# Stick-breaking sums from two rounded halves, a later sparse tail, and an early start of the mixing-out projection

## The chip, the cores and the metric

The kernel is one program on one core of a Trainium2 chip. The metric is the device time of one execution in microseconds; the time before is the median of three runs. Its engines are TensorE (PE, with the weight load PEld), VectorE (DVE), ScalarE (ACT), GpSimd (POOL) and SyncE (SP).

## The reference, cut to what matters

Two transformer blocks run in f32 on 512 tokens of width 1024. The change lies in the second, in its attention stage. There, eight heads do sparse attention and eight do stick-breaking attention; both outputs are joined and projected:

```python
def stick_breaking(q, k, v):                       # 8 heads of 64
    z = jnp.einsum('bhqd,bhkd->bhqk', qb, k) * scale      # qb: 128 queries
    mask = kpos[None, :] < tq[:, None]
    log_rem = jnp.where(mask, jax.nn.log_sigmoid(-z), 0.0)
    suffix = lax.cumsum(log_rem, axis=3, reverse=True) - log_rem
    a = jnp.where(mask, jnp.exp(jax.nn.log_sigmoid(z) + suffix), 0.0)
    return jnp.einsum('bhqk,bhkd->bhqd', a, v)

x = x + jnp.concatenate([o_nsa, o_sb], axis=-1) @ w_out
x = x + memory_cross_attention(rms_norm_2(x, ...), ...)
```

Since log_sigmoid(z) = z - softplus(z), the exponent is z minus the sum of softplus over this key and all later ones. With keys on the partitions that sum is a product of a triangle of minus ones with the softplus values of the same block of 128 keys, plus a product of a full block of minus ones with those of each later block.

## The kernel before, in words

Activations lie transposed, features on the partitions, as eight chunks `[128, 512]`. A projection multiplies in three rounded products (fp32r), high by high, low by high and high by low (`mm3`, L415 to L417): `xh`, `xl` are the halves of the activations, `wh`, `wl` those of the weights. ScalarE makes the high half of a weight unit (L341), VectorE the low half (L353); both work one unit ahead. Semaphores order the engines, and each engine runs its instructions in the order in which they are written.

The attention stage is `pe_second_attention`, `act_second_attention` and `dve_second_attention` (from L2203). One loop over `s` runs first over 24 sparse jobs, then over ten stick-breaking units, with `n = s - 24`. A sparse job passes through scores (step s), turn (s + 1: products with a diagonal, L688, then copies, L707 and L714) and attend (s + 2, L723); the last of three jobs is put into `xh` and `xl` (L730, L733). These outputs fill chunks 0 to 3, those of stick-breaking 4 to 7.

A stick-breaking unit holds, for two heads, four blocks of keys by 128 queries, thus 1024 columns: query block 3 of one pair of heads, or blocks 0 and 2 of one pair, or block 1 of two pairs. Among the ten units there are four, four and two of these. The order on TensorE in round n is

- scores(n): 16 small products (L2089) and the mask (L2094), into one of three pairs of banks (0 and 1, 2 and 3, 4 and 5); they wait for the exponential of unit n - 3, which reads the same banks;
- sums(n - 2): f32 products of minus ones with the later blocks (L2143, L2147) and with the triangle (L2148), added onto the scores;
- attend(n - 3): 16 products with the values (L2172) into bank 6 or 7, waiting for the VectorE put of unit n - 5.

ScalarE in round n: absolute value of scores(n) (L2103), exponential of unit n - 2 (L2157), the two steps of the log for n (L2107, L2109), the high-half put of unit n - 4 (L730). VectorE: softplus of n (L2121), the additions of later blocks (L2128 to L2133; two, one or none), the low-half put of unit n - 4 (L733).

`pe_mix_out` (L1228) then multiplies eight output tiles c of 128 features, each of eight chunks by three products of 512 columns, in banks 0 and 1 by turns. For tile c it waits for the residual addition of tile c - 2 (L738). The first block's mixing-out ("out") already starts with chunks 0 to 3 beside the attention; the second's ("out2") does not. `pe_memory` follows, with its two query projections in banks 2 and 3.

Of the kernel before, what the change touches and what calls it, by code (L numbers as in the profile page):

```python
# [7 lines left out]
ALU = mybir.AluOpType  # L8
# [151 lines left out]
def program(nc, A, out, tables):  # L160
    ctx = ExitStack()
    with ctx:
# [115 lines left out]
        pr2 = sb("pr2", [P, 2, 4, T], F32, part)  # L278
        pt2 = sb("pt2", [P, 2, 4 * T], F32, part)
        part.close()  # L280
        second.close()
# [944 lines left out]


        def pe_mix_out(e, name, stage):  # L1228
            for n in range(4):
                u = of[name, n]  # L1230
                e.wait_ge(*WLO[u])
                for cc in range(2):
                    c = 2 * n + cc
                    if c > 1:
                        e.wait_ge(*VF[name, "residual", c - 2])
                    k0 = 4 if n == 0 and name == "out" else 0
                    pe_proj(e, c % 2, u, cc * P, xh, xl, stage if c == 0 else None, NC - k0, k0, k0 == 0, kw=k0).then_inc(
                        *MM.up((name, "out", c), *([("w", u)] if cc else [])))
                pe_finish(e, u)
# [9 lines left out]
        def dve_mix_out(e, name, coef, each=None):  # L1249
            for n in range(4):  # L1250
                dve_ahead(e, of[name, n])
                for c in (2 * n, 2 * n + 1):
                    dve_residual(e, name, c, c % 2, coef(c))
# [857 lines left out]
        def dve_stick_logs(e, n):  # L2111

            par = n % 2
            e.wait_ge(*EX["log", n])
            if n < 2:
# [3 lines left out]
            i, o = (3, 0) if len(STICK[n]) == 1 else (2, P)  # L2119
            last = [("stick", "sums", n)]  # L2120
            e.scalar_tensor_tensor(out=zs[par], in0=stick_scores(n), scalar=0.0, in1=ze[par], op0=ALU.max, op1=ALU.add).then_inc(  # L2121
                *VS.up(("stick", "soft", n), *(last if STICK[n][0][1] == 1 else [])))
            if STICK[n][0][1] == 1:
                return
            z, u = (x[par].rearrange("p (y t) -> p y t", y=2) for x in (zs, zu))
            e.wait_ge(*VS["stick", "soft", n])
            if i == 3:
                e.tensor_tensor(u[:, :, P:2 * P], z[:, :, 2 * P:3 * P], z[:, :, 3 * P:4 * P], ALU.add).then_inc(  # L2128
                    *VS.up(("stick", "later", n)))
                e.wait_ge(*VS["stick", "later", n])  # L2130
                e.tensor_tensor(u[:, :, 0:P], z[:, :, P:2 * P], u[:, :, P:2 * P], ALU.add).then_inc(*VS.up(*last))
            else:
                e.tensor_tensor(u[:, :, 0:P], z[:, :, 2 * P:3 * P], z[:, :, 3 * P:4 * P], ALU.add).then_inc(*VS.up(*last))  # L2133

        def pe_stick_sums(e, n):
            par = n % 2
            e.wait_ge(*VS["stick", "sums", n])
            for y in range(2):
                s, z = (x[:, y * 512:(y + 1) * 512] for x in (stick_scores(n), zs[par]))
                u = zu[par][:, y * 256:(y + 1) * 256]  # L2140
                for c, i, o in stick_entries(n):
                    if i > 1:
                        e.matmul(s[:, o:o + (i - 1) * P], b2("neg1"), u[:, 0:(i - 1) * P], start=False, stop=False,  # L2143
                                 skip_group_check=True)
                    if i:
                        a = o + (i - 1) * P
                        e.matmul(s[:, a:a + P], b2("neg1"), z[:, a + P:a + 2 * P], start=False, stop=False, skip_group_check=True)  # L2147
                m = e.matmul(s, b2("tri"), z, start=False, stop=True, skip_group_check=True)  # L2148
            m.then_inc(*MM.up(("stick", n)))
# [42 lines left out]
        def dve_stick_put(e, n):  # L2192
            dst, src = stick_places(n, xl)
            e.wait_ge(*AX["stick", n])
            dve_put(e, dst, src, stick_places(n, xh)[0], ("stick", n), *([("mix2", c) for c in range(NC)] if n == NU - 1 else []))

# [6 lines left out]
        def pe_second_attention(e):  # L2203
# [4 lines left out]
            for s in range(NN + NU + 3):  # L2208
# [7 lines left out]
                elif 2 <= n < NU + 2:  # L2216
                    pe_stick_sums(e, n - 2)
                if 1 < s < NN + 2:
                    J = nsa_[s - 2]
                    if J.first and J.n:  # L2220
                        e.wait_ge(*VX["nsa", J.n - 1, 1])
                    pe_attend(e, J)
                elif n >= 3:
                    pe_stick_attend(e, n - 3)

        def act_second_attention(e):
            for s in range(NN + NU + 4):
# [11 lines left out]
                if 0 < s <= NN:  # L2239
                    act_turn(e, nsa_[s - 1])  # L2240
                if 1 < s < NN + 2:
                    J = nsa_[s - 2]
                    if J.last:
# [7 lines left out]
        def dve_second_attention(e):  # L2251
            for s in range(NN + NU + 4):
# [7 lines left out]
                if s < NN:  # L2260
                    dve_scale(e, nsa_[s])
                if 1 < s < NN + 2:
                    J = nsa_[s - 2]
                    if J.last:
                        for o in range(2):
                            r, cs, cols, src = nsa_places(J, o)
                            e.wait_ge(*AX["nsa", J.n, o])
                            dve_put(e, xl[r, cs, cols], src, xh[r, cs, cols], ("nsa", J.n, o))
                elif n >= 4:
# [23 lines left out]
        def pe_memory(e):  # L2293
            u = of["mq"]
            e.wait_ge(*WLO[u])
            pe_proj(e, 2, u, 0, nh, nl, "n5").then_inc(*MM.up(("in2", "qm0")))
            e.wait_ge(*VF["square", "out2", 7])
            pe_sums(e, "out2", ssum, 1, T)
            pe_proj(e, 3, u, P, nh, nl, nk=4, stop=False)
            pe_head_sums(e, "qm0", 0, 8, VF["token term", "out2"])  # L2300
            pe_proj(e, 3, u, P, nh, nl, nk=4, k0=4, kw=4, start=False).then_inc(*MM.up(("in2", "qm1"), ("w", u)))
            pe_head_spread(e, "qm0", 1, T, 6)
# [33 lines left out]
        def act_memory(e):  # L2336
            act_head_in(e, "qm0", 2, qm[:, 0, :], 0)
            act_head_root(e, "qm0", 1)
            act_ahead(e, of["mq"])
            act_head_in(e, "qm1", 3, qm[:, 1, :], 1)  # L2340
            act_head_root(e, "qm1", 2)
# [288 lines left out]
```

## Time and profile before

| | us |
|---|---|
| median of three runs (2232.75 to 2236.04) | 2235.04 |
| the profiled execution | 2237.97 |
| its span, first to last instruction | 2236.1 |
| stretch from the first stick-breaking scores to the first mixing-out product | 1709.1 to 1776.4 |

The span and all the rows are of the one profiled execution. A row of the timeline gives start, length and line; several instructions of one kind are merged (x16). The length of a TensorE row includes the time in which its last product drains, so that the next row begins before it ends: the step from start to start is the time that the array takes. The time in brackets is idle time before, and what ended it.

### The profile page before, as it was taken

The numbers are of one execution on the slowest core, as the hardware profiler recorded it, in microseconds if no ns is written. First come the engines' busy times: TensorE is split into PE (matmuls) and PEld (weight loads), VectorE is DVE, ScalarE is ACT, GpSimd is POOL, SyncE is SP. The second block draws the span as 40 slices with busy tenths as digits, with TensorE's granted clock in tenths as the row PEclk, the third lists the DMA queues.
The fourth block names the chain that finished last, engine by engine and source line by source line (L and its number), as shares of the span: only waits on it lengthen the run. The fifth ranks groups of instructions, "written<-read, shape, count | busy, mean of one in ns | idle before, by whom it ended". The sixth has DMA issues, their size and how long they took to land.

```text
span 2236.1 us, 26468 instructions
## 1 busy us (share of the span) xinstructions
PE 2163.9 (97%) x11362; PEld 1776.0 (79%) x11362; DVE 1049.0 (47%) x1381; ACT 746.4 (33%) x1125; POOL 78.5 (4%) x76
## 2 busy tenths in 40 slices
PE   6989989999998999999999999999999999999999
PEld 4778778888887888888888888877777677888887
DVE  5758565555536333333533333363375357333322
ACT  4335332222233222232322322333356545222211
POOL 0000000000000000000111100000000002111000
PEclk9999999999998999999999999999899999999999
DMA  9421445555531333323233323333100021333232
GB/s 356 132 83 39 151 132 191 190 170 196 179 105 57 94 94 101 100 86 109 87 102 94 95 85 104 104 92 113 57 1 1 20 75 57 94 100 105 93 96 78
DMA packets 190901, 236.03 MB, mean 106 GB/s; under 512 B 4096, under 2 KB 175392, under 8 KB 190656
## 3 DMA queue, kind: packets, MB, share of 16 engines
q1 hardware_dynamic: 189696, 230.42, 32.1%
q0 software_dynamic: 1088, 3.92, 0.5%
q8 instruction: 90, 1.47, 0.3%
q14 instruction: 27, 0.22, 0.0%
HBM read 231.31 MB, written 2.10 MB: 104 GB/s over the span
## 4 chain that ended last, share of the span: by engine, by line
PE 86%; DVE 6%; ACT 4%; DMA 1%; SPq 1%; issue 1%; DVEq 0%; ACTq 0%
PE ps L415 25%; PE ps L417 25%; PE ps L416 25%; PE ps L688 3%; PE ps L618 2%; PE ps L723 1%; ACT pr L647 1%; DVE wl L353 1%; SPq L782 1%; PE ps L394 1%; DVE tmp L547 1%; ACT wh L341 1%; PE ps L508 1%; DMA mmT<-in_ada_w 1%; PE ps L459 1%
## 5 line engine op out<-in xcount | busy, mean ns | idle before, releaser
L415 PE MATMUL ps<-xh,wh 128*128 128x512 f32 x1768 | 697.7, 395 | 17.7 <-DVE xl L559 8.0
L416 PE MATMUL ps<-xl,wh 128*128 128x512 f32 x1768 | 691.4, 391 | 0.0
L417 PE MATMUL ps<-xh,wl 128*128 128x512 f32 x1768 | 691.3, 391 | 0.0
L353 DVE TENSOR_TENSOR wl<-raw,wh 128x2048 fp32r<-128x2048 f32 (+2 forms) x169 | 376.8, 2230 | 488.7 <-ACT wh L341 488.6
L341 ACT CAST wh<-raw 128x2048 fp32r<-128x2048 f32 (+1 forms) x170 | 314.5, 1850 | 339.9 <-PE ps L417 254.0
L415 PEld LDWEIGHTS ps<-xh,wh 128*128 128x128 f32 x1768 | 333.2, 188 | 93.5 <-issue 14.6
L417 PEld LDWEIGHTS ps<-xh,wl 128*128 128x128 f32 x1768 | 333.0, 188 | 70.7
L416 PEld LDWEIGHTS ps<-xl,wh 128*128 128x128 f32 x1768 | 333.2, 188 | 70.1 <-issue 1.4
L415 PE MATMUL ps<-hh,wh 128*128 128x512 f32 x704 | 274.3, 390 | 0.0
L417 PE MATMUL ps<-hh,wl 128*128 128x512 f32 x704 | 274.1, 389 | 0.0
L416 PE MATMUL ps<-hl,wh 128*128 128x512 f32 x704 | 274.1, 389 | 0.0
L1351 ACT CAST hh<-tmp 128x512 fp32r<-128x512 f32 x88 | 54.7, 621 | 328.7 <-DVE tmp L1405 328.7
L417 PEld LDWEIGHTS ps<-hh,wl 128*128 128x128 f32 x704 | 132.2, 188 | 27.4
L415 PEld LDWEIGHTS ps<-hh,wh 128*128 128x128 f32 x704 | 132.2, 188 | 27.3
L416 PEld LDWEIGHTS ps<-hl,wh 128*128 128x128 f32 x704 | 132.2, 188 | 27.2
L1405 DVE TENSOR_TENSOR tmp<-ps,tmp 128x512 f32<-128x512 f32 x88 | 60.8, 691 | 140.3 <-PE ps L417 137.2
L367 DVE SCALAR_TENSOR_TENSOR acc<-raw,sc,acc 128x1024 f32<-128x1024 f32 x70 | 89.9, 1284 | 40.7 <-DMA raw<-in_ada_w 39.2
L688 PE MATMUL ps<-tmp,pr 128*128 128x128 f32 (+1 forms) x736 | 98.2, 290 | 5.1 <-DVE tmp L671 4.1
L647 ACT ACTIVATE pr<-ps,sm 128x512 f32<-128x512 f32 (+5 forms) x144 | 72.6, 513 | 80.0 <-DVE sm L634 44.5
L688 PEld LDWEIGHTS ps<-tmp,pr 128*128 128x128 f32 (+1 forms) x736 | 89.0, 193 | 9.0 <-DVE tmp L671 5.9
L733 DVE TENSOR_TENSOR hl<-tmp,hh 128x512 fp32r<-128x512 f32 x88 | 60.9, 693 | 60.5 <-ACT hh L1351 60.5
L1432 POOL TENSOR_TENSOR tmp<-tmp,acc 128x512 f32<-128x512 f32 x44 | 56.8, 1292 | 802.3 <-ACT tmp L1333 802.3
(345 smaller groups left out, 1765.3 us busy)
## 6 DMA issues: line engine op xcount, KB each, us to landing
raw<-in_ffn_w SPq DMA_DIRECT2D x52, 1024.0 KB, 5.5
raw<-in_ada_w SPq DMA_DIRECT2D x40, 1024.0 KB, 5.4
raw<-in_ffn_wg SPq DMA_DIRECT2D x22, 1024.0 KB, 5.5
raw<-in_ffn_wu SPq DMA_DIRECT2D x22, 1024.0 KB, 5.3
raw<-in_ffn_w SPq DMA_DIRECT2D x16, 896.0 KB, 4.8
raw<-in_ffn_wd SPq DMA_DIRECT2D x16, 896.0 KB, 5.1
raw<-in_w_in SPq DMA_DIRECT2D x10, 1024.0 KB, 5.3
raw<-in_ffn_wd SPq DMA_DIRECT2D x8, 1024.0 KB, 5.2
```

The lines of the kernel that those rows point to most:

```text
L341: e.copy(wh[k % 2][:, 0:n], raw[i % 2][:, 0:n]).then_inc(*WHI.up(i))
L353: e.tensor_tensor(wl[s][:, 0:n], r[:, 0:n], wh[s][:, 0:n].bitcast(F32), ALU.subtract).then_inc(*WLO.up(i))
L367: e.scalar_tensor_tensor(out=acc[:, :], in0=w, scalar=col, in1=acc[:, :], op0=ALU.mult, op1=ALU.add).then_inc(*VA.up((i, kk), *([i, ("sum" ...
L415: e.matmul(dst, ah, bh, start=start, stop=False)
L416: e.matmul(dst, ah, bl, start=False, stop=False)
L417: return e.matmul(dst, al, bh, start=False, stop=stop)
L647: e.activation(prs[J.name][:, J.par, g, 0:J.width], ps[:, o:o + J.width], ACT.Exp, bias=m, accum_out=sm[:, J.par, 4 + g:5 + g]).then_inc(* ...
L688: m = e.matmul(bank[0:w, o:o + P], prs[J.name][:, J.par, g, col:col + w], diagonal(J)[:, g], start=True, stop=True, skip_group_check=True)
L733: e.tensor_tensor(dst, src, high.bitcast(F32), ALU.subtract).then_inc(*VX.up(*keys))
L1351: e.copy(hidden[f][0][:, i, :], tmp[i % 2][:, :]).then_inc(*AX.up((f, i)))
L1405: e.tensor_tensor(t, pb[2 + cc], t, ALU.mult).then_inc(*VF.up(("up", f, i)))
L1432: e.tensor_tensor(t, t, rsx, ALU.mult).then_inc(*GP.up(("gate", f, i)))
```

## The change

The sums of stick-breaking: VectorE still makes softplus, now into two chunks of `q2`; then it copies it rounded (`zh`) and subtracts (`zl`). TensorE multiplies each half by minus ones and by the triangle, both rounded from a constant copied once (`stick_tri`), in single-pass products; the later blocks are one product for each distance d instead of VectorE's additions. The high half's products wait for the copy, the low half's for the subtraction.

The attend and the puts of the last sparse job move from round n = 1 to n = 2, behind the sums of unit 0. And tiles 0 and 1 of mixing-out multiply chunks 0 to 3 in rounds n = 11 and 12, between the sums of unit 9 and attend(8), and between that and attend(9), in banks 2 and 3; the memory queries take banks 0 and 1.

```diff
+        stick_tri = sb("stick_tri", [P, P + 2], F32R, second)
+        zhl = sb("zhl", [P, 2, 4 * T], F32R, part)      # over pr2
+        def pe_out_ahead(e, c):
+            if c > 1:
+                return
+            u = of["out2", 0]
+            if c == 0:
+                e.wait_ge(*WLO[u])
+                e.wait_ge(*EX["stick", NU - 3])
+            pe_proj(e, 2 + c, u, c * P, xh, xl, "mix2" if c == 0 else None, 4, stop=False)
...
-                    k0 = 4 if n == 0 and name == "out" else 0
-                    pe_proj(e, c % 2, u, ...
+                    k0 = 4 if n == 0 else 0
+                    pe_proj(e, c % 2 + (2 if name == "out2" else 0), u, ...
...
-        zs = [pr2[:, par].rearrange("p g t -> p (g t)")[:, 0:1024] for par in range(2)]
-        zu = [pr2[:, par].rearrange("p g t -> p (g t)")[:, 1024:1536] for par in range(2)]
+        zs = q2[:, 0:2, :].rearrange("p c t -> p (c t)")
+        zh, zl = ([zhl[:, par, o:o + 1024] for par in range(2)] for o in (0, 1024))
...  dve_stick_logs
-            e.scalar_tensor_tensor(out=zs[par], ...
-            ... two, one or no tensor_tensor additions into zu
+            e.scalar_tensor_tensor(out=zs, in0=stick_scores(n), scalar=0.0, in1=ze[par], op0=ALU.max, op1=ALU.add)
+            e.tensor_copy(zh[par], zs).then_inc(*VS.up(("stick", "high", n)))
+            e.wait_ge(*VS["stick", "high", n])
+            e.tensor_tensor(zl[par], zs, zh[par].bitcast(F32), ALU.subtract).then_inc(*VS.up(("stick", "low", n)))
...  pe_stick_sums
+            neg = stick_tri[:, P:P + 1].broadcast_to([P, P])
+            for w, half in enumerate((zh[par], zl[par])):
+                e.wait_ge(*VS["stick", "low" if w else "high", n])
+                for y in range(2):
+                    s, z = (x[:, y * 512:(y + 1) * 512] for x in (stick_scores(n), half))
+                    for c, i, o in stick_entries(n):
+                        for d in range(1, i + 1):
+                            e.matmul(s[:, o:o + (i + 1 - d) * P], neg, z[:, o + d * P:o + (i + 1) * P], ...)
+                    m = e.matmul(s, stick_tri[:, 0:P], z, ...)
...  second_attention, on TensorE, ScalarE and VectorE
-                if 1 < s < NN + 2:
-                    J = nsa_[s - 2]
+                if 1 < s < NN + 1 or n == 2:
+                    J = nsa_[min(s - 2, NN - 1)]
...  on TensorE, after the sums
+                if n >= NU + 1:
+                    pe_out_ahead(e, n - NU - 1)
...  on VectorE
+                if s == 12:
+                    e.tensor_copy(stick_tri[:, :], b2("tri", P + 2)).then_inc(*VF.up("stick triangle"))
...  pe_memory, act_memory
-            pe_proj(e, 2, ...) and 3, act_head_in bank 2 and 3
+            pe_proj(e, 0, ...) and 1, act_head_in bank 0 and 1
```

## Rows read from the trace of the kernel before

**Rows 1.** The page, part 1: busy time of each engine, share of the span, instructions

```profile
PE 2163.9 (97%) x11362; PEld 1776.0 (79%) x11362; DVE 1049.0 (47%) x1381; ACT 746.4 (33%) x1125; POOL 78.5 (4%) x76
```

**Rows 2.** Windows view: busy us (instructions) per engine, granted clock, DMA share, GB/s

```profile
1709.00:1776.40 67.40, 61.28 (x538) 42.69 (x537) 23.80 (x40) 45.63 (x56) 0.00 (x0) 1.00 0.00 1
```

**Rows 3.** Timeline of TensorE, two rounds: start us, us, line, operation, shapes

```profile
1731.44 1.16 PE L2089 MATMUL ps<-qsT,ksbT 64*128 64x128 f32 x16
1732.77 0.65 PE L2143 MATMUL ps<-pr,acc 128*128 128x256 f32 x2
...
1735.94 1.09 PE L2172 MATMUL ps<-pt,vsb 128*64 128x128 f32 x16
1737.13 1.16 PE L2089 MATMUL ps<-qsT,ksbT 64*128 64x128 f32 x16
...
1738.34 0.44 PE L2143 MATMUL ps<-pr,acc 128*128 128x128 f32 x2
...
1741.10 1.09 PE L2172 MATMUL ps<-pt,vsb 128*64 128x128 f32 x16
```

**Rows 4.** Timeline of ScalarE: the exponential of unit 2

```profile
1736.05 1.02 ACT L2157 ACTIVATE pt<-ps 128x1024 f32<-128x1024 f32 x1 [1.62 <-PE ps L2148]
```

**Rows 5.** Timeline of VectorE: softplus of units 4 and 5, and a put

```profile
1739.23 1.22 DVE L2121 SCALAR_TENSOR_TENSOR pr<-ps,C2S 128x1024 f32<-128x1024 f32 x1 [4.00 <-ACT C2S L2109]
...
1744.39 1.23 DVE L2121 SCALAR_TENSOR_TENSOR pr<-ps,pt 128x1024 f32<-128x1024 f32 x1 [3.74 <-ACT pt L2109]
...
1746.45 0.42 DVE L733 TENSOR_TENSOR xl<-ps,xh 128x256 fp32r<-128x256 f32 x1
```

**Rows 6.** Waits view, 1700 to 1780 us: total us, times, longest

```profile
PE ps L2172 <- DVE xl L733: 2.8, 4, 1.0
```

**Rows 7.** Timeline of TensorE: first and 60th product of mixing-out

```profile
1776.42 0.47 PE L415 MATMUL ps<-xh,wh 128*128 128x512 f32 x1 [1.01 <-DVE xl L733]
...
1789.88 0.39 PE L417 MATMUL ps<-xh,wl 128*128 128x512 f32 x1
```

**Rows 8.** Timeline of TensorE: 36 rounded products of 256 columns, first and last

```profile
1589.75 0.28 PE L415 MATMUL ps<-wh,xh 128*128 128x256 f32 x1
...
1593.95 0.28 PE L417 MATMUL ps<-wh,xl 128*128 128x256 f32 x1
```

**Rows 9.** Timeline of TensorE: eight products of two columns, and the next

```profile
1829.14 0.95 PE L459 MATMUL ps<-cst,tmp 128*128 128x2 f32 x8
1829.95 0.48 PE L415 MATMUL ps<-nh,wh 128*128 128x512 f32 x1
```

**Rows 10.** Groups of weight loads: busy us, mean ns, idle before

```profile
L508 PEld LDWEIGHTS ps<-cst,hs 128*64 128x64 f32 x144 | 8.2, 142 | 3.6 <-DVE hs L499 1.9 <-issue 0.9 <-DVE kmT L573 0.8
```

**Rows 11.** Groups of VectorE by shape: busy us, mean ns, idle before

```profile
L364 DVE TENSOR_SCALAR acc<-raw,sc 128x1024 f32<-128x1024 f32 x10 | 7.5, 748 | 0.0
...
L353 DVE TENSOR_TENSOR wl<-raw,wh 128x1024 fp32r<-128x1024 f32 x1 | 1.2, 1226 | 0.7 <-ACT wh L341 0.7
```

**Rows 12.** Timeline of TensorE: last sparse attend, and scores of unit 3

```profile
1718.72 1.95 PE L723 MATMUL ps<-pt,v2w 128*64 128x256 f32 x16
...
1726.17 1.16 PE L2089 MATMUL ps<-qsT,ksbT 64*128 64x128 f32 x16 [1.11 <-ACT pt L2157]
```

**Rows 13.** Timeline of VectorE: puts of the last sparse job

```profile
1723.76 0.87 DVE L733 TENSOR_TENSOR xl<-ps,xh 64x256 fp32r<-64x256 f32 x2
```

**Rows 14.** Timeline of TensorE: attend of the last unit

```profile
1774.32 1.09 PE L2172 MATMUL ps<-pt,vsb 128*64 128x128 f32 x16 [0.66 <-DVE xl L733]
```

**Rows 15.** Timeline of VectorE: low half of mixing-out's second weights

```profile
1777.66 2.29 DVE L353 TENSOR_TENSOR wl<-raw,wh 128x2048 fp32r<-128x2048 f32 x1 [1.38 <-ACT wh L341]
```

**Rows 16.** Windows view: a lull of TensorE, and the clock behind it

```profile
168.00:170.00 2.00, 0.00 (x0) 0.00 (x0) 1.67 (x4) 1.84 (x6) 0.00 (x0) 1.00 0.86 262
170.00:172.00 2.00, 1.92 (x16) 1.44 (x16) 1.24 (x5) 1.10 (x5) 0.00 (x0) 0.63 0.76 263
172.00:174.00 2.00, 2.00 (x13) 1.83 (x12) 1.36 (x3) 0.29 (x1) 0.00 (x0) 0.52 0.00 0
```

More of the change, by code:

```diff
@@ L279, in program @@
         pt2 = sb("pt2", [P, 2, 4 * T], F32, part)
+        part.close()
+        part = ExitStack()
+        zhl = sb("zhl", [P, 2, 4 * T], F32R, part)
         part.close()
@@ L2114, in dve_stick_logs @@
             e.wait_ge(*EX["log", n])
+            if n == 0:
+                e.wait_ge(*EX["nsa", NN - 1, 3])
+            else:
+                e.wait_ge(*VS["stick", "low", n - 1])
+            e.scalar_tensor_tensor(out=zs, in0=stick_scores(n), scalar=0.0, in1=ze[par], op0=ALU.max, op1=ALU.add).then_inc(
+                *VS.up(("stick", "soft", n)))
             if n < 2:
@@ L2118, in dve_stick_logs @@
                 e.wait_ge(*MM["stick", n - 2])
[L2119 to L2125, printed above, removed]
@@ L2126, in dve_stick_logs @@
-            e.wait_ge(*VS["stick", "soft", n])
[L2127 to L2133, printed above, removed]
+            e.wait_ge(*VS["stick", "soft", n])
@@ L2135, in pe_stick_sums @@
+            e.tensor_copy(zh[par], zs).then_inc(*VS.up(("stick", "high", n)))
+            e.wait_ge(*VS["stick", "high", n])
+            e.tensor_tensor(zl[par], zs, zh[par].bitcast(F32), ALU.subtract).then_inc(*VS.up(("stick", "low", n)))
         def pe_stick_sums(e, n):
             par = n % 2
[L2137 to L2148, printed above, removed]
+            neg = stick_tri[:, P:P + 1].broadcast_to([P, P])
@@ new lines, in pe_stick_sums @@
+            if n == 0:
+                e.wait_ge(*VF["stick triangle"])
+            for w, half in enumerate((zh[par], zl[par])):
[4 more added lines that the diff above has]
+                        for d in range(1, i + 1):
+                            e.matmul(s[:, o:o + (i + 1 - d) * P], neg, z[:, o + d * P:o + (i + 1) * P], start=False, stop=False,
+                                     skip_group_check=True)
+                    m = e.matmul(s, stick_tri[:, 0:P], z, start=False, stop=w == 1, skip_group_check=True)
@@ L2194, in dve_stick_put @@
             e.wait_ge(*AX["stick", n])
-            dve_put(e, dst, src, stick_places(n, xh)[0], ("stick", n), *([("mix2", c) for c in range(NC)] if n == NU - 1 else []))
+            dve_put(e, dst, src, stick_places(n, xh)[0], ("stick", n), *([("mix2", c) for c in range(4, NC)] if n == NU - 1 else []))
         def nsa_places(J, o):
@@ L2240, in act_second_attention @@
                     act_turn(e, nsa_[s - 1])
-                if 1 < s < NN + 2:
-                    J = nsa_[s - 2]
+                if 1 < s < NN + 1 or n == 2:
+                    J = nsa_[min(s - 2, NN - 1)]
                     if J.last:
@@ L2267, in dve_second_attention @@
                             e.wait_ge(*AX["nsa", J.n, o])
-                            dve_put(e, xl[r, cs, cols], src, xh[r, cs, cols], ("nsa", J.n, o))
+                            dve_put(e, xl[r, cs, cols], src, xh[r, cs, cols], ("nsa", J.n, o),
+                                    *([("mix2", c) for c in range(4)] if o and J.n == NN - 1 else []))
                 elif n >= 4:
@@ L2295, in pe_memory @@
             e.wait_ge(*WLO[u])
-            pe_proj(e, 2, u, 0, nh, nl, "n5").then_inc(*MM.up(("in2", "qm0")))
+            pe_proj(e, 0, u, 0, nh, nl, "n5").then_inc(*MM.up(("in2", "qm0")))
             e.wait_ge(*VF["square", "out2", 7])
             pe_sums(e, "out2", ssum, 1, T)
-            pe_proj(e, 3, u, P, nh, nl, nk=4, stop=False)
+            pe_proj(e, 1, u, P, nh, nl, nk=4, stop=False)
             pe_head_sums(e, "qm0", 0, 8, VF["token term", "out2"])
-            pe_proj(e, 3, u, P, nh, nl, nk=4, k0=4, kw=4, start=False).then_inc(*MM.up(("in2", "qm1"), ("w", u)))
+            pe_proj(e, 1, u, P, nh, nl, nk=4, k0=4, kw=4, start=False).then_inc(*MM.up(("in2", "qm1"), ("w", u)))
             pe_head_spread(e, "qm0", 1, T, 6)
@@ L2336, in act_memory @@
         def act_memory(e):
-            act_head_in(e, "qm0", 2, qm[:, 0, :], 0)
+            act_head_in(e, "qm0", 0, qm[:, 0, :], 0)
             act_head_root(e, "qm0", 1)
             act_ahead(e, of["mq"])
-            act_head_in(e, "qm1", 3, qm[:, 1, :], 1)
+            act_head_in(e, "qm1", 1, qm[:, 1, :], 1)
             act_head_root(e, "qm1", 2)
```

8 lines of the change are left out of this document (4 added, 4 removed).

## The prediction

> **What bounds the kernel now.** I read the busy line of the page first. It says TensorE 97% [rows 1]: whatever shortens the kernel must shorten TensorE's work or fill its gaps. The change touches one stretch, from the last sparse job to the first product of the mixing-out projection (1709.1 to 1776.4 us). The windows view there shows TensorE busy 61.28 of 67.4 us at full granted clock, and ScalarE 45.6, VectorE 23.8 [rows 2]. At most 6 us are idle, so the rest must come from work taken off.
>
> The timeline of TensorE then gives one round of the stick-breaking loop, which is scores(n), sums(n-2), attend(n-3) [rows 3]. Scores take 1.33 us (1731.44 to 1732.77), or 1.21 for a unit with one entry (1737.13 to 1738.34). Sums take 3.17 and 2.76 us. Attend takes 1.09, and 0.10 passes until the next scores may start, because they overwrite the bank that ScalarE's last exponential reads. Two rounds take 5.69 and 5.16 us, mean 5.42.
>
> A second loop runs beside it, over two rounds. I follow it from the exponential of unit k. ScalarE then makes the logs of unit k+2; VectorE starts 3.18 us after the exponential (1736.05 to 1739.23) [rows 4, 5]. VectorE's softplus and sums of later blocks take 2.06 us until the put of unit k-2 can start (1744.39 to 1746.45); with one addition instead of two it is some 1.6. The put takes 0.42 at most. Attend(k) waits for that put: the waits view has four such waits, 2.8 us together [rows 6]. Then 1.09 attend, some 1.27 scores, the sums of k+2, some 0.2 for handovers, and the next exponential. With a long addition and short sums: 3.18 + 2.06 + 0.42 + 0.05 + 1.09 + 1.27 + 2.72 + 0.2 = 11.0; for two rounds that is 5.5 each. So TensorE's own work (5.42) and the loop through ScalarE and VectorE (5.5) are about tied. That is what I rest on: relieving one of two tied bounds yields little, and lengthening the other costs at once.
>
> **Part 1, the sums' products.** Before, each f32 product is two passes. After, each rounded product is one pass, but there are two halves, and the "later blocks" are one product per distance, without VectorE's additions. Prices: 512 columns, rounded: 59 steps from 1776.42 to 1789.88, 0.228 each [rows 7]. 256 columns: 35 steps from 1589.75 to 1593.95, 0.120 each [rows 8]. 384 lies between: 0.173. A rounded product of 128 columns does not occur. From below, the line through the two gives 0.067; from above, the f32 price: sums of 2.76 us over 2 x 768 columns [rows 3] make 0.23 for 128. I take 0.105: a f32 weight block of this size with two moving columns takes 0.101 [rows 9], so the weight load, not the columns, is the nearest bound. The Trainium skill (TensorE: Matmul & The Clock Gate, Back-to-back issue gap) gives about 81 ns for a sustained pair of weight load and product at 128 columns, shorter than these rows; by that page the sum below would be some 0.7 us lower, an estimate.
>
> Per unit and both halves: block 3: 4 x (0.228 + 0.173 + 0.120 + 0.105) = 2.50, was 3.17. Blocks 0 and 2: 4 x (0.228 + 0.120 + 0.105) = 1.81, was 2.7. Two blocks 1: 4 x (0.228 + 0.210) = 1.75, was 2.7. Over 4, 4 and 2 units TensorE loses 2.7 + 3.6 + 1.9 = 8 us of work. The weight of the later blocks is one column broadcast over 128. The spreads load such weights now, 142 ns for 64 columns [rows 10], hidden like any load; I add nothing, and were it dearer, the narrow products would show it first, as in rival A. The triangle's copy at job 12 (one VectorE operation, under 0.3 us) hides behind TensorE there.
>
> **Part 2, VectorE's side.** Softplus stays 1.23. The additions (0.83, 0.42 or nothing) go. In comes a copy of 1024 columns, SBUF to SBUF: a scalar multiply of that shape takes 0.748 [rows 11], I take 0.72; the bounds are 0.5, a third below that row, and 1.23, one element at a time as softplus. Then a subtraction of 1024 columns, 1.226 by [rows 11], I take 1.20. The low half is ready 1.26 + 0.72 + 0.03 + 1.20 = 3.21 us after softplus starts, and the put queued behind it starts at 3.13 instead of 2.06 or 1.6. TensorE may start the high half's products at 1.98, but that is never late; the put is.
>
> New bounds per round: TensorE 1.09 + 1.27 + 2.15 + 0.1 = 4.6. The loop: 3.18 + 3.13 + 0.34 + 0.05 + 1.09 + 1.27 + 2.15 + 0.2 = 11.4, so 5.7. The loop now decides alone, and is 0.2 to 0.3 longer per round than the tie before. From the exponential of unit 0 to that of unit 8 there are eight rounds. I stepped the dependencies through with these prices (the same stepping with the old prices ends the stretch at 1776.6, the trace at 1776.42): by it 42.7 us before, 44.3 after, **+1.6**. The 8 us of TensorE work turn into gaps ahead of attend.
>
> **Part 3, the sparse tail.** Now attend of the last sparse job stands at 1718.72, ahead of the scores of unit 2 and the sums of unit 0, and TensorE later idles 1.11 us at 1726.17 waiting for the first exponential [rows 12]. Moved one round back, scores(2) start at 1718.6, the sums of unit 0 end at 1722.4, and the exponential starts near 1722.9 instead of 1725.1 (1726.17 less its own 1.07): **-2.2** (1.9 the moved attend, the rest the cheaper sums). The price comes later: its puts on ScalarE and VectorE (the latter 0.87 us, [rows 13]) now queue behind the logs of unit 2. Attend(0) waits for them: exponential(0) 1722.92, logs(2) done 1726.1, low half 1729.3, puts 1730.1. TensorE has finished the sums of unit 1 by 1727.4 and idles 2.7 us. This gap is in the +1.6. By the same stepping part 3 with the new sums loses 1.3 against leaving the tail where it was; with the old sums it would win 1.1.
>
> **Part 4, mixing-out's first half.** 24 products (5.44 us) go ahead of attend(8) and attend(9). They add nothing, being taken from the products after; they fill the 0.66 us gap at 1774.32. The 1.01 us before 1776.42 stays, since the last unit's put still comes after the last attend [rows 7, 14]. That wins 0.65. Their banks 2 and 3 were read by exponential 7, long done, and the first weights have lain ready since the sv projections. Behind them, output tile 2 is due 5.4 us after the products begin, not 10.9; its weights' low half ends 3.5 us after (1779.95 against 1776.42) [rows 15], so 1.9 us are left. Last part, exponential 8 to product start with the 5.44 taken off: 8.6 before, 8.8 after, **+0.2**, the 0.65 included: attend(7) now waits 2.9 us for put(5), behind the low half of unit 9. Moving the memory queries' banks costs nothing; they are only swapped.
>
> **Sum.** -2.2 + 1.6 + 0.2 = -0.4; with the stepping's own start and end unrounded -0.6. I take -0.5. The profiled execution took 2237.97 (span 2236.1) and would be 2237.5; the median shown is 2235.04, so I predict 2234.5. About 0.2%, 4.5 us, is what a measurement of this kernel can tell from no change.
>
> **The rivals.**
> A, *the narrow product is dear*: 0.23 instead of 0.105. There are 48, about 28 of them in the loop that decides: +3.5, so +3.0, 2238.0, slower. It turns to a loss from 0.125 on. For it: no row has the shape; against: the weight row. A copy at single rate (1.2 us) belongs here; it alone would bring the sum to +1.4, and with both it is +4.9.
> B, *the clock falls*: at 168 to 170 TensorE stood idle 2 us and was granted 0.63 of its clock in the next two us and 0.52 in the two after, which is its 1.2 GHz level [rows 16]: 4 x (1 - 0.575) = 1.7 us of array time lost. The change makes three gaps of 2.5 to 2.9 us (before attend 0, 2, 7) where none passed 1.11 and the clock stayed at 1.00. If one to three of them bring such a stretch, all inside the loop, that is +1.7 to +5.1, so +1.2 to +4.6; if the low clock holds for longer, up to +8. It decides if the gaps are there at all. Likeliest 2238.5, slower. The Trainium skill (TensorE: Matmul & The Clock Gate, HAM oscillation) says too that a gap between bursts of products can bring the low clock back; the trace agrees in that [rows 16].
> C, *TensorE's work alone decides*: then 8 us of products, 1.1 of the gap at 1726 and 0.65 go: -9.7, 2225.3. For it: TensorE 97% busy; against: the four waits of attend for a put, which stand in the very loop that gets longer.
>
> **How the numbers follow.** Forecast 0.60, own range 2232 to 2237 (0.067 and a 0.5 copy: -2.4; executions scatter by 1.5). A 0.12, B 0.20, C 0.08. Faster by over 0.2%: nearly all of C and a trace of the rest, 0.09. Slower: 0.10 from B, 0.03 from A with a dear copy, 0.13. Within: 0.78. Range 2231 to 2240: it leaves out C and B's far end.
>
> **What would show it.** Right: the exponential of unit 0 starts 2.2 us earlier; rounds of 5.7 us; TensorE waits 2 us and more for puts ahead of attend(0), (2), (7); VectorE's three operations run 3.2 us; sums take 2.5, 1.8 and 1.8 us; the gap ahead of attend(9) is gone and the last 1.0 us is there. Wrong: rounds near 4.7 us (C), sums of 3 us (A), a granted clock under 1.00 between 1709 and 1776 (B), or a wait ahead of output tile 2.

## The result, and the profile after

| | before | after |
|---|---|---|
| median of 20 runs | 2234.56 | 2240.97 |
| lowest and highest | 2227.94, 2240.45 | 2235.82, 2245.01 |
| the profiled execution | 2237.97 | 2238.87 |
| its span | 2236.1 | 2237.1 |

The ratio is 1.0029, with an interval of 1.0021 to 1.0038: slower by 6.4 us, where the forecast was a gain of 0.5 us, too small to measure. The median is 1 us above the top of the forecast's range.

The two spans are only 1.0 us apart, and they must not be compared whole. Between 1595 and 1619 us, well ahead of the change, the execution of before was granted less clock than that of after. Windows view of before, with the columns of [rows 2]:

```profile
1595.00:1619.00 24.00, 21.93 (x132) 15.03 (x131) 11.80 (x43) 10.86 (x47) 0.00 (x0) 0.64 0.00 1
```

and of after:

```profile
1595.00:1619.00 24.00, 21.41 (x167) 14.64 (x167) 15.73 (x58) 13.18 (x63) 0.00 (x0) 0.86 0.01 1
1703.32:1783.93 80.61, 68.02 (x578) 55.93 (x577) 37.73 (x48) 45.89 (x56) 0.00 (x0) 0.89 0.00 1
```

0.64 against 0.86 of 24 us is 5.3 us, and the stick-breaking stage starts 5.8 us earlier after (1703.32 against 1709.10). That is scatter between two executions: up to there the two kernels differ by nothing but one small VectorE copy. So from here on I measure the *stretch*: from the first stick-breaking scores to the first mixing-out product behind the last unit, less 5.44 us where 24 products were done ahead of it. Before it is 67.32 us at clock 1.00 (window of [rows 2], cut exactly). After, by the second line above, it is 80.61 - 5.44 = 75.17 us at clock 0.89: **+7.85**.

TensorE's busy line falls by only 4.8 us against [rows 1], though 8 us of products are gone:

```profile
PE 2159.1 (97%) x11378; PEld 1780.1 (80%) x11378; DVE 1062.6 (48%) x1390; ACT 747.2 (33%) x1125; POOL 78.4 (4%) x76
```

The timeline of TensorE in the stretch answers to [rows 3, 12, 14]. Here are the gaps ahead of attend, what stands behind two of them, one unit's sums, and the last gap:

```profile
1714.85 0.51 PE L2156 MATMUL ps<-zhl,stick_tri 128*128 128x384 f32 x3
1715.20 0.45 PE L2158 MATMUL ps<-zhl,stick_tri 128*128 128x512 f32 x1
1715.48 0.51 PE L2156 MATMUL ps<-zhl,stick_tri 128*128 128x384 f32 x3
...
1724.55 1.54 PE L2182 MATMUL ps<-pt,vsb 128*64 128x128 f32 x16 [2.44 <-DVE xl L737]
1726.03 2.08 PE L2103 MATMUL ps<-qsT,ksbT 64*128 64x128 f32 x16
...
1738.07 1.41 PE L2182 MATMUL ps<-pt,vsb 128*64 128x128 f32 x16 [2.46 <-DVE xl L737]
1739.41 2.08 PE L2103 MATMUL ps<-qsT,ksbT 64*128 64x128 f32 x16
...
1742.48 0.33 PE L2156 MATMUL ps<-zhl,stick_tri 128*128 128x128 f32 x2
1742.65 0.44 PE L2158 MATMUL ps<-zhl,stick_tri 128*128 128x512 f32 x1
1742.93 0.33 PE L2156 MATMUL ps<-zhl,stick_tri 128*128 128x128 f32 x2
...
1750.85 1.09 PE L2182 MATMUL ps<-pt,vsb 128*64 128x128 f32 x16 [1.77 <-DVE xl L737]
...
1763.81 1.09 PE L2182 MATMUL ps<-pt,vsb 128*64 128x128 f32 x16 [1.79 <-DVE xl L737]
...
1768.88 1.50 PE L2182 MATMUL ps<-pt,vsb 128*64 128x128 f32 x16 [1.93 <-DVE xl L737]
...
1783.93 0.47 PE L419 MATMUL ps<-xh,wh 128*128 128x512 f32 x1 [1.02 <-DVE xl L737]
```

Five gaps of 1.77 to 2.46 us end with a VectorE put (the waits view sums them to 10.4 us, where [rows 6] had 2.8). Behind the first two, the same sixteen scores products take 2.08 us instead of 1.16: that is not waiting, that is the array at its lower level. The windows view shows it, with the columns of [rows 16]:

```profile
1726.00:1728.00 2.00, 2.00 (x18) 1.79 (x16) 1.86 (x3) 0.00 (x0) 0.00 (x0) 0.50 0.00 0
1728.00:1730.00 2.00, 2.00 (x16) 1.87 (x15) 0.62 (x1) 1.03 (x1) 0.00 (x0) 0.89 0.03 8
...
1754.00:1756.00 2.00, 2.00 (x10) 1.81 (x10) 1.89 (x3) 1.02 (x1) 0.00 (x0) 0.56 0.00 0
...
1770.00:1772.00 2.00, 2.00 (x10) 1.60 (x7) 0.00 (x0) 0.00 (x0) 0.00 (x0) 0.50 0.00 0
1772.00:1774.00 2.00, 2.00 (x8) 1.71 (x8) 0.00 (x0) 0.00 (x0) 0.00 (x0) 0.50 0.00 0
1774.00:1776.00 2.00, 2.00 (x6) 1.53 (x5) 0.29 (x1) 1.18 (x2) 0.00 (x0) 0.50 0.00 0
```

0.50 of the clock is the 1.2 GHz level. Added up over all two-us windows, 2 x (1 - clock), the stretch lost 8.54 us of array time in four falls: 1.70 behind the gap at 1724.55, 1.72 behind 1738.07, 1.70 behind 1750.85, and 3.42 behind 1768.88. Before, it lost 0.00.

These are figures of one execution each. The mean granted clock of the whole kernel, which is on record for every execution, says the same: its median is 0.985 in the 20 executions of after and 0.988 in the 29 of before that ran beside e1 to e4. A difference of 0.003 over 2238 us is 6.7 us of array time (the clock is given to 0.001, so to some 2 us), and the medians differ by 6.4. The two profiled executions alone have 0.986 both, since this one of before lost elsewhere what after lost in the stretch.

The chain of waits says why attend is late. This piece leads from the logs of unit 2 to attend(0) (start us, us, what):

```profile
1719.16 1.16 ACT C2S L2123
1720.32 0.02 issue
1720.34 1.24 DVE q L2133
...
1721.67 0.70 DVE zhl L2140
...
1722.40 1.22 DVE zhl L2142
1723.62 0.06 DVE xl L737
...
1723.98 0.44 DVE xl L737
1724.42 0.14 issue
1724.55 1.54 PE ps L2182 x16
```

Softplus, copy and subtraction (L2133, L2140, L2142) of unit 2 stand ahead of the put (L737) on which attend(0) waits. VectorE is 47% busy there (37.73 of 80.61 us): it isn't short of time, the put is short of a place in its queue.

### The profile page after: what moved, and what is told of

It is laid out like the page before. It is cut to its first block, busy times and chain, and to the rows that moved or that the text cites. A ratio compares the mean times of both kernels' runs of the same rounds, so it can differ in the third digit from the quotient of the medians.

```text
span 2237.1 us, 26521 instructions
## 1 busy us (share of the span) xinstructions
PE 2159.1 (97%) x11378; PEld 1780.1 (80%) x11378; DVE 1062.6 (48%) x1390; ACT 747.2 (33%) x1125; POOL 78.4 (4%) x76
## 4 chain that ended last, share of the span: by engine, by line
PE 85%; DVE 7%; ACT 4%; DMA 1%; SPq 1%; issue 1%; DVEq 0%; ACTq 0%
PE ps L419 25%; PE ps L420 25%; PE ps L421 25%; PE ps L692 3%; PE ps L622 2%; ACT pr L651 1%; PE ps L727 1%; DVE wl L357 1%; SPq L786 1%; PE ps L398 1%; DVE tmp L551 1%; ACT wh L345 1%; PE ps L512 1%; DMA mmT<-in_ada_w 1%; PE ps L463 1%
## 5 line engine op out<-in xcount | busy, mean ns | idle before, releaser
L737 DVE TENSOR_TENSOR hl<-tmp,hh 128x512 fp32r<-128x512 f32 x88 | 60.9, 692 | 60.5 <-ACT hh L1365 60.5
```

The lines of the kernel that those rows point to most:

```text
L737: e.tensor_tensor(dst, src, high.bitcast(F32), ALU.subtract).then_inc(*VX.up(*keys))
```

## Experiments

Two theories for the +7.85. **Clock**: the gaps themselves cost what was forecast, and some 7 us are products at half speed behind them. **Waits**: the longer loop through VectorE costs all of it, and the low clock only fills time that would be waited away anyway. A third question is the order of the put in VectorE's queue.

Stretch, "lost" (array time lost to the clock, as above) and waits are of one profiled execution each. The medians are of 12 executions (e1, e2, e3), 11 (e5), 10 (e8), 6 (e4) or 5 (e7, e10), each beside executions of before.

| kernel | stretch, us | lost, us | waits of attend, us | median, its before | ratio (interval) |
|---|---|---|---|---|---|
| before | 67.32 | 0.00 | 2.8 | | |
| after | 75.17 | 8.54 | 10.4 | 2240.97, 2234.56 | 1.0029 (1.0021 to 1.0038) |
| e1 sums only | 69.81 | 3.42 | 8.6 | 2237.47, 2235.08 | 1.0017 (1.0005 to 1.0030) |
| e2 old sums, rest new | 65.95 | 0.00 | 2.5 | 2234.13, 2235.08 | 0.9996 (0.9987 to 1.0006) |
| e3 filler | 68.08 | 0.00 | 2.7 | 2236.03, 2235.08 | 1.0003 (0.9994 to 1.0012) |
| e4 puts between | 61.47 | 1.72 | 2.9 | 2227.26, 2235.08 | 0.9964 (0.9950 to 0.9978) |
| e5 no tail | 69.31 | 3.40 | 7.9 | 2238.38, 2234.59 | 1.0020 (1.0010 to 1.0029) |
| e7 puts first | 57.36 | 0.00 | 0.4 | 2222.82, 2234.59 | 0.9953 (0.9939 to 0.9966) |
| e8 before, puts first | 64.78 | 0.00 | 0.0 | 2230.93, 2234.59 | 0.9983 (0.9971 to 0.9995) |
| e10 between, ahead 10 | 58.04 | 0.00 | 1.2 | 2225.10, 2234.59 | 0.9958 (0.9946 to 0.9971) |

**e3: fill the gaps.** The same kernel as after, with 77 products more that nobody reads, on TensorE in front of attend's wait: 18, 16, 12, 6, 7 and 18 ahead of attend 0, 2, 4, 5, 6 and 7. The real work and its order stay.

```diff
+        FILL = {0: 18, 2: 16, 4: 12, 5: 6, 6: 7, 7: 18}
...  pe_stick_attend, ahead of the wait
+            for x in range(FILL.get(n, 0)):
+                m = e.matmul(pb[6 + (n + 1) % 2][:, 256:512], b_("ident"), b_("ident", 256), ...)
+                ... the last one: then_inc(*ST.up(("fill", n)))
             e.wait_ge(*EX["stick", n])
...  act_stick_put
+            if n + 1 in FILL:
+                e.wait_ge(*ST["fill", n + 1])
```

> The changed kernel, with products that nobody uses in TensorE's gaps ahead of attend: 18, 16, 12, 6, 7 and 18 bf16 products of 256 columns (0.11 us each) ahead of attend 0, 2, 4, 5, 6 and 7, into columns of the other attend bank that nothing reads (ScalarE's next put of that bank waits for them). No wait that existed is taken away. Theory (of the 7.9 us lost in the stretch, 8 are lost to the half clock, the waits themselves cost nothing net): granted clock 1.00 in the stretch, stretch 67 to 68 instead of 75.2, time within 0.1% of before, some 7 us faster than the changed kernel. Rival (the waits cost by themselves and the low clock only lies beside them): stretch stays at 74 to 76, whatever the clock.

Timeline of TensorE, the filler ahead of attend(0) (0.12 us a product), then the windows view of the stretch of the same kernel:

```profile
1726.58 2.14 PE L2173 MATMUL ps<-bcs 128*128 128x256 bf16 x18
```

```profile
1707.95:1781.47 73.52, 68.66 (x655) 56.62 (x654) 37.78 (x48) 46.10 (x56) 0.00 (x0) 1.00 0.01 1
```

TensorE now does *more* (655 instructions against 578), and the stretch is 7.09 us shorter, 68.08, at clock 1.00. Against its own runs of before, the median is +0.95 us, where after stood at +6.4. The mean clock of the whole kernel goes from 0.985 to 0.9875 (median of 12 executions). So the clock theory holds, and the waits theory falls: 7.1 of the 7.85 us are the four falls, and all the rest (waits longer, products shorter) nets 0.76. The waits are not free: they eat the 8 us of products that were taken off, and in e3 the filler only stands in their place. Between the 8.54 lost and the 7.1 gained stand 1.4 us; that they fell in time that TensorE would have waited anyway is argued, not tested.

**e1: sums alone.** After, with the tail and the mixing-out products back in their old places.

```diff
-                    k0 = 4 if n == 0 else 0
-                    pe_proj(e, c % 2 + (2 if name == "out2" else 0), u, ...
+                    k0 = 4 if n == 0 and name == "out" else 0
+                    pe_proj(e, c % 2, u, ...
...
-                if n >= NU + 1:
-                    pe_out_ahead(e, n - NU - 1)
-                if 1 < s < NN + 1 or n == 2:
-                    J = nsa_[min(s - 2, NN - 1)]
+                if 1 < s < NN + 2:
+                    J = nsa_[s - 2]
```

> Only the sums are changed: rounded halves as in the changed kernel, but the last sparse job's attend and puts stay where they were before, and mixing-out starts after the last unit. 'Stretch' is from the first stick-breaking scores to the first product of mixing-out behind the last unit, less the products already done: 67.3 us before, 75.2 in the changed kernel (1703.32 to 1783.93, less 5.44). Theory (the clock falls behind the gaps ahead of attend): stepping the dependencies at full clock gives 66.3; three gaps of 1.8 to 2.9 us stay (attend 2, 4, 7), each followed by a stretch at half clock that loses 1.7 us or more: stretch 69 to 72, granted clock under 0.96, about +3 us or 0.1 to 0.2% slower than before. Rival (the moved tail is what makes it slow, the sums win): stretch 66 and clock 1.00, 1 us faster. Rival (the waits alone, whatever the clock): stretch over 72 at clock 1.00.

+2.49 in the stretch, with two falls, and +2.4 in the median: the new sums by themselves already lose. Timeline of TensorE, its gaps:

```profile
1738.18 1.09 PE L2182 MATMUL ps<-pt,vsb 128*64 128x128 f32 x16 [2.46 <-DVE xl L737]
...
1749.42 1.09 PE L2182 MATMUL ps<-pt,vsb 128*64 128x128 f32 x16 [1.73 <-DVE xl L737]
...
1762.39 1.09 PE L2182 MATMUL ps<-pt,vsb 128*64 128x128 f32 x16 [1.79 <-DVE xl L737]
...
1767.45 1.85 PE L2182 MATMUL ps<-pt,vsb 128*64 128x128 f32 x16 [1.93 <-DVE xl L737]
```

```profile
1740.00:1742.00 2.00, 2.00 (x22) 1.75 (x19) 1.86 (x3) 1.03 (x1) 0.00 (x0) 1.00 0.00 0
...
1752.00:1754.00 2.00, 2.00 (x15) 1.68 (x12) 1.86 (x3) 0.97 (x1) 0.00 (x0) 0.51 0.00 0
```

The longest gap, 2.46, brought no fall (clock 1.00 at 1740); that of 1.73 did, and that of 1.79 did not. A gap's length alone does not tell whether the clock falls. I had expected three gaps and a fall behind each; there were four gaps and two falls.

**e2: the two moves with the old sums.** Before, with the tail and the mixing-out products moved as in after.

```diff
-                if 1 < s < NN + 2:
-                    J = nsa_[s - 2]
+                if n >= NU + 1:
+                    pe_out_ahead(e, n - NU - 1)
+                if 1 < s < NN + 1 or n == 2:
+                    J = nsa_[min(s - 2, NN - 1)]
```

> The other two parts without the first: f32 sums and VectorE additions as before, with the sparse tail moved back and mixing-out's first half ahead. Theory (the loss comes from the two VectorE operations of the new sums and the gaps behind them): no gap of TensorE over 1.5 us, clock 1.00, stretch 65.6 by the stepping (1.1 from the tail, 0.65 from the products ahead), 0.1% faster than before, hardly measurable. Rival (the moved tail's puts, queued behind the logs of unit 2, make the first gap and the clock falls there also with the old sums): a gap over 2 us ahead of attend(0) and stretch 67 or more.

-1.37 in the stretch, no fall, no gap over 0.96 us but the last; the median (-0.95, interval of the ratio across 1) can't tell that from no change. The moves are sound with the old sums.

**e5: after without the moved tail.**

```diff
-                if 1 < s < NN + 1 or n == 2:
-                    J = nsa_[min(s - 2, NN - 1)]
+                if 1 < s < NN + 2:
+                    J = nsa_[s - 2]
```

> The changed kernel with the last sparse job's attend and puts back at round n = 1; the new sums and the products ahead stay. Theory (clock falls behind gaps; the moved tail makes one of them, ahead of attend(0)): that gap goes, those ahead of attend(2), (4), (6), (7) stay; by the stepping at full clock 0.65 less than the kernel with only the new sums, whose stretch was 69.8, so 69 to 70, clock 0.94 to 0.96, against 75.2 of the changed kernel. The moved tail then costs 5 to 6 us with the new sums, though it gained with the old ones (65.95 against 67.3 with the products ahead). Rival (the products ahead add to the loss, since they stand ahead of attend(8) and (9)): stretch 72 or more.

In the profiled executions the stretch is 5.86 us shorter without the moved tail (75.17 to 69.31), and 5.1 of them are two falls fewer (8.54 - 3.40). All executions together show less: the median went from +6.4 to +3.8, the intervals of the two ratios overlap, and the mean clock of the whole kernel is no higher (0.984 in 11 executions, against 0.985). So that the moved tail loses with the new sums is likely, and that it costs as much as 5.86 us is not shown. Against e1, the products ahead gain 0.50 (69.81 - 69.31).

**e4: the put between softplus and copy.** After, with VectorE's put of unit n - 4 (and the last sparse put) between the softplus and the copy of unit n, not behind the subtraction.

```diff
-        def dve_stick_logs(e, n):
+        def dve_stick_logs(e, n, between=None):
...  behind softplus
+            if between:
+                between()
             e.wait_ge(*VS["stick", "soft", n])
...
-                    dve_stick_logs(e, n)
+                    dve_stick_logs(e, n, (lambda: dve_nsa_put(nsa_[NN - 1])) if n == TAIL == 2 else
+                                   (lambda: dve_stick_put(e, n - 4)) if n >= 4 else None)
...
-                elif n >= 4:
+                elif n >= NU:
                     dve_stick_put(e, n - 4)
```

> The changed kernel with VectorE's put of unit n-4 (for n = 2 that of the last sparse job) between the softplus of unit n and its copy, instead of behind the subtraction. Theory (attend waits for puts behind the low half; that makes the gaps, and they bring the low clock): puts start 1.2 us after softplus instead of 3.1; gaps ahead of attend shrink to under 0.8 us except ahead of attend(7), 2.0; clock 1.00 or one fall; the 8 us of TensorE work taken off come out: stretch 59 at full clock, 61 with one fall, so 6 to 8 us or 0.3 to 0.4% faster than before. Rival (the half clock comes from too little TensorE work per time, not from the gaps): clock under 0.95 again, stretch 65 or more. Rival (the loop through ScalarE and VectorE decides anyway): stretch 66 to 67 at full clock.

The same products and copies, only the order on VectorE changed: the stretch is 13.7 us shorter than after's and the kernel 7.8 us faster than before. Of the 13.7, 6.8 are array time no longer lost to the clock (8.54 to 1.72), and 6.9 are the rest, for the most part waiting (the waits of attend go from 10.4 to 2.9). One long gap is left, and the only fall comes behind it. Timeline of TensorE, and windows:

```profile
1754.07 1.09 PE L2185 MATMUL ps<-pt,vsb 128*64 128x128 f32 x16 [1.73 <-DVE xl L737]
```

```profile
1756.00:1758.00 2.00, 2.00 (x8) 1.81 (x8) 0.12 (x1) 0.00 (x0) 0.00 (x0) 0.50 0.00 0
```

**e10: fill that gap with real work.** e4, with the two mixing-out tiles in rounds 10 and 12 in place of 11 and 12. The diff is against e4.

```diff
-                if n >= NU + 1:
-                    pe_out_ahead(e, n - NU - 1)
+                if n in (NU, NU + 2):
+                    pe_out_ahead(e, (n - NU) // 2)
```

> The kernel with VectorE's puts between softplus and copy (stretch 61.47, one fall of the clock behind the 1.73 us gap ahead of attend(7)), with the first mixing-out tile moved up into that gap (round 10; the second in round 12). Theory (that gap is what let the clock fall): gap gone, clock 1.00, stretch 57 to 58 (2.1 for the gap, 1.7 or more for the clock), 0.45% under before. Rival (the fall came from elsewhere): clock 0.97 again and stretch over 59.

58.04, 3.4 us less than e4 (1.7 less of waits, 1.72 less lost to the clock); the 2.2 us less of the median can't be told from none (the intervals of the two ratios overlap). The mean clock of the whole kernel is 0.987 in both. In the profiled execution the same products as in the change, put where the gap is, fill it, and the clock stays at 1.00.

**e7: puts first.** e10's placing, and the puts ahead: ScalarE's behind the absolute value of scores(n), VectorE's ahead of softplus(n). The sparse put stays between softplus and copy of unit 2, as in e4. The diff is against e10.

```diff
                     act_stick_abs(e, n)
+                if n >= 4:
+                    act_stick_put(e, n - 4)
...
-                    dve_stick_logs(e, n, (lambda: dve_nsa_put(nsa_[NN - 1])) if n == TAIL == 2 else
-                                   (lambda: dve_stick_put(e, n - 4)) if n >= 4 else None)
+                    if n >= 4:
+                        dve_stick_put(e, n - 4)
+                    dve_stick_logs(e, n, (lambda: dve_nsa_put(nsa_[NN - 1])) if n == TAIL == 2 else None)
...  the puts in their old place go
```

> The version that the runs point to: the changed kernel with ScalarE's put of unit n-4 right behind the absolute values of n and VectorE's ahead of softplus n (the sparse job's put between softplus 2 and its copy), and the first of mixing-out's two tiles ahead in round 10, ahead of attend(7), the second in round 12. Theory (gaps, and behind them the low clock, are all that stands against the 8 us of work taken off): no gap over 1 us but the known ones, clock 1.00, stretch 56.4 by the stepping (67.3 - 11.2 + 0.3), time 0.5% under before, 2224. Rival (the loop through ScalarE and VectorE decides in any order of puts): stretch 60 or more at clock 1.00. Rival (a fall of the clock comes anyway): clock under 0.98, stretch 59 to 61.

The fastest of all: 2222.82, 11.8 us faster than before (0.9953, 0.9939 to 0.9966); the stretch, 57.36, is 1.0 longer than expected. Its interval overlaps with those of e4 and e10. Windows view of its stretch, where TensorE is busy 60.04 of 62.80 us:

```profile
1705.07:1767.87 62.80, 60.04 (x579) 49.38 (x577) 37.74 (x48) 45.52 (x56) 0.00 (x0) 1.00 0.00 1
```

**e8: the order of the puts alone.** Before, with the old sums, tail and mixing-out, and the same two moves of the puts.

```diff
                     act_stick_abs(e, n)
+                if n >= 4:
+                    act_stick_put(e, n - 4)
...
-                elif n < NU:
-                    dve_stick_logs(e, n)
+                else:
+                    if n >= 4:
+                        dve_stick_put(e, n - 4)
+                    if n < NU:
+                        dve_stick_logs(e, n)
...  the puts in their old place go
```

> The kernel before with nothing changed but the order of the puts: ScalarE's behind the absolute values, VectorE's ahead of softplus. Theory (before, TensorE's own work of 5.42 us a round and the loop of 5.5 were about tied, so freeing the loop yields only the small waits): the waits of attend for puts (2.8 us) go, stretch 65 by the stepping (-2.3), clock 1.00, 0.1% faster, at the edge of what can be measured. Rival (the puts' order is worth as much there as in the changed kernel, 13 us): stretch under 62.

64.78, -2.54: all four waits of [rows 6] (2.8 us) are gone, and the median is 3.7 us lower. Timeline of TensorE, the only wait for a put that is left:

```profile
1768.99 0.47 PE L415 MATMUL ps<-xh,wh 128*128 128x512 f32 x1 [1.02 <-DVE xl L733]
```

With the puts first, the new sums, the tail and mixing-out's tiles (in rounds 10 and 12) are worth 7.4 us in the stretch (64.78 to 57.36); with the puts last the change cost 7.85.

## Why the prediction was wrong, step by step

**What bounds the kernel: right.** TensorE's work and the loop through the puts were about tied: e8 relieves the loop alone and wins only 2.5 us of 67.

**Part 1, the products: right in sum.** The products of one rounded half with one half of the columns (each unit has four such groups): 0.63 us for block 3 (1714.85 to 1715.48), forecast 0.626; 0.45 for two blocks 1 (1742.48 to 1742.93), forecast 0.438. Two narrow products take 0.17 (1742.48 to 1742.65), so 0.085 each and not 0.105; the triangle's 512 columns take 0.28 (1715.20 to 1715.48) and not 0.228. The two errors cancel. Rival A is out. Where the saving comes from: before, one f32 product of the triangle with 512 columns stands in the trace as two instructions, 0.86 us together from start to start (1722.52 to 1723.38); the two rounded ones take 0.56.

**Part 2, VectorE's side: right in size.** Timeline of VectorE, the round of unit 2, which answers to [rows 5, 13]:

```profile
1720.34 1.23 DVE L2133 SCALAR_TENSOR_TENSOR q<-ps,C2S 128x1024 f32<-128x1024 f32 x1 [0.67 <-ACT C2S L2123]
1721.67 0.69 DVE L2140 CAST zhl<-q 128x1024 fp32r<-128x1024 f32 x1
1722.40 1.22 DVE L2142 TENSOR_TENSOR zhl<-q,zhl 128x1024 fp32r<-128x1024 f32 x1
1723.54 0.87 DVE L737 TENSOR_TENSOR xl<-ps,xh 64x256 fp32r<-64x256 f32 x2
```

The copy takes 0.69 (forecast 0.72), the subtraction 1.22 (1.20), and the put starts 3.20 us behind softplus (3.13). The Trainium skill (VectorE: DVE Perf Modes, The perf-mode tier table) says that an op with one f32 source can run at double rate when all is in SBUF, and one with two sources cannot; 0.69 against 1.22 agrees, here with a rounded output. The exponentials tell what it made of a round. With the clock held (e3) they run 45.16 us from unit 0 to unit 8, against 42.71 before: +2.45, where +1.6 was forecast. That is 5.65 per round, the 5.7 of the forecast's loop; its stepping had 44.3, or 5.54, and was the worse of the two. After itself has 49.82, another 4.7 that go when the clock is held.

**Part 3, the tail: right in its first half.** The first exponential comes 13.84 us into the stretch, was 16.00: -2.16, forecast -2.2. The gap ahead of attend(0) is 2.44, forecast 2.7. The move's worth with the new sums was put at a loss of 1.3; the profiled executions differ by 5.86 (e5), 0.7 of them without the clock. The forecast priced a gap as its length alone, and a low spell follows this one.

**Part 4, mixing-out: nearly right.** The 0.66 ahead of attend(9) is gone, the last 1.02 stays, output tile 2 starts without a wait, the gain is 0.50 (e1 against e5) for 0.65. From exponential 8 to the product behind the last unit, less the 5.44, it was 8.61 us before and is 9.08 with the clock held (e3): +0.47, forecast +0.2.

**The sum: -2.16 + 2.45 + 0.47 = +0.76 at full clock, by e3, where -0.5 stood.** Most of the difference is in the loop (2.45 for 1.6). By itself this error of 1.3 us stays within the own range of the forecast (2232 to 2237). It is not what made it wrong.

**The step that failed: the clock was put at nothing in the sum, and left to rival B.** The forecast had the new gaps ahead of attend(0), (2) and (7), took their length into the +1.6, and added no term for what the clock does behind them. The runs show that term: 8.54 us of array time in four falls, 7.09 us of the stretch (after against e3), against +0.76 for all that the sum did hold. The mechanism stood in rival B, with the price of one fall, 1.7 us, read from [rows 16]. That price was right: of the nine falls in the stretches of after, e1, e4 and e5, eight cost 1.70 to 1.72 us. Two things were wrong.

First, the count: I counted gaps of 2.5 us and more, one to three of them. There were five of 1.77 us and more (2.44, 2.46 and 1.93 ahead of attend 0, 2 and 7, and two that I had not listed, ahead of attend 4 and 6). Four of them brought a fall, and the last spell was twice as long. With 4 falls at 1.7 my sum would have been +6.3; measured are +7.85 in the stretch and +6.4 in the median.

Second, the chance, 0.20, for something whose condition my own forecast contained. Once the forecast says that the new gaps are there, the low clock behind them is a term of the sum. [rows 16] spoke for it, and no gap in the stretch of before, all of 1.11 us or less, spoke against it. The rest of that trace, which the forecast did not use, speaks for counting gaps shorter than 2.5 us too, but not for certainty. Timeline of TensorE before, two of its gaps, and the windows view behind each:

```profile
82.81 0.71 PE L508 MATMUL ps<-cst,hs 128*128 128x128 f32 x4 [2.25 <-DVE hs L499]
...
1501.27 0.50 PE L415 MATMUL ps<-xh,wh 128*128 128x512 f32 x1 [1.59 <-DVE wl L353]
```

```profile
84.00:86.00 2.00, 2.00 (x10) 1.63 (x10) 1.81 (x6) 1.31 (x3) 0.00 (x0) 1.00 0.89 282
...
1502.00:1504.00 2.00, 2.00 (x6) 1.61 (x5) 0.39 (x1) 1.99 (x3) 0.00 (x0) 0.50 0.75 178
```

Behind the gap of 2.25 us the clock stayed, behind that of 1.59 it fell. And the gap of [rows 16] itself, 2.50 us long, is there in after too, in the same code, without a fall. Timeline and windows view of after:

```profile
169.50 0.37 PE L622 MATMUL ps<-kT,qT 64*128 64x128 f32 x1 [2.51 <-ACT pr L651]
```

```profile
170.00:172.00 2.00, 2.00 (x25) 1.67 (x24) 1.77 (x6) 0.52 (x3) 0.00 (x0) 1.00 0.37 129
```

So whether a given gap brings a fall differs from one execution to the next, and the count in one trace is in part luck. That the new gaps cost clock on the whole is not: the mean clock over all executions (0.988 before, 0.985 after) shows it. The Trainium skill (TensorE: Matmul & The Clock Gate, HAM oscillation) says that gaps between bursts of products can bring the low clock back again and again; here that is four falls in 80 us, all behind waits for VectorE and none behind a DMA.

**Rival C** was priced at -9.7 for the case that TensorE's work alone decides. It failed here because of the puts' place and the clock behind the gaps that this makes; with the puts first and a tile in round 10 (e7) the stretch is 9.96 us shorter than before's.

**Open:** why some gaps bring no fall. Of the fourteen gaps of 1.72 to 2.46 us in the stretches of after, e1, e4 and e5, nine did. In after the gap of 1.79 at 1763.81 did not, that of 1.77 at 1750.85 did; in e1 and e5 that of 2.46 did not. The filler of e3 and the tile of e10 shorten the gaps and give TensorE more to do at once, so they do not tell whether the length of a gap or the amount of work around it counts. Nothing in the profile that I read separates the gaps.

## What to carry to other kernels

Before putting work onto an engine that also carries small hand-overs, look at what is queued behind it: here 1.9 us of copy and subtraction a unit, on an engine half idle, stood ahead of the hand-over, and the kernel lost 6.4 us; with the hand-over between softplus and copy the same work gained 7.8 us (e4), and 11.8 with the puts first and a tile moved as well (e7). Price a new gap of TensorE as its length plus a possible spell at half clock behind it (1.7 us and more here), even for gaps under 2 us. And where a gap can't be avoided, move real products into it.

## What the runs showed of the hardware that was not expected

- Gaps of 1.59 to 2.50 us in otherwise busy work brought the lower level (1501.27 before; 1724.55 and others after; [rows 16]), but not each of them, and the same gap not in each execution (170.08 before, 169.50 after).
- The low spell behind 1768.88 cost 3.42 us, twice each of the others, though TensorE was busy 2.00 of every 2.00 us from 1770 on (window rows above). Other spells cost more: in the trace of before, 5.1 us of array time from 283 us on, 6.8 from 689 on and 8.5 from 1600 on. The last is the stretch from 1595 to 1619 with a mean clock of 0.64; e4 runs the same work there and loses nothing. Windows view of e4:

```profile
1595.00:1619.00 24.00, 20.99 (x184) 14.30 (x182) 16.41 (x61) 14.43 (x72) 0.00 (x0) 1.00 0.01 1
```

- Products whose results nobody reads kept the clock at 1.00 in the stretch, and 77 of them took 5.5 us off the kernel's loss (+6.4 to +0.95).
- The product with the triangle, which stands between products with the broadcast column, steps 0.28 us for 512 columns (1715.20 to 1715.48), against 0.228 in mixing-out [rows 7], where weights are loaded for each product too.
